# An expert's outputs added to the result: VectorE straight from PSUM, or a ScalarE copy and a GpSimd addition

## What is computed

```python
def moe_swiglu(h, router, w_gate_up, w_down):      # h: 256 tokens x 1024
    logits = hf @ router
    top_v, top_i = lax.top_k(logits, 2)
    gates = jax.nn.softmax(top_v, axis=-1)
    combine = sum(one_hot(top_i, 8) * gates[..., None])
    for e in range(8):                             # D_FF_EXPERT = 3584
        gate, up = split(hf @ w_gate_up[e])
        out = out + combine[:, e:e+1] * ((silu(gate) * up) @ w_down[e])
x = layer_norm(ALPHA * x + out + ple, ln2_g, ln2_b)
```

## Time and profile before

| | us |
|---|---|
| median of 3 runs | 1656.19 (1654.77 to 1656.62) |
| profiled execution, its time | 1656.22 |
| profiled execution, its span | 1654.0 |
| PE busy | 1591.2 (96% of the span) |
| DVE busy | 1356.8 (82%) |
| ACT busy | 979.7 (59%) |
| POOL busy | 164.3 (10%) |

### The profile page before, as it was taken

One profiled execution on the slowest core, in us unless ns is written; L12 is line 12 of the kernel. 1 busy time (PEld: TensorE's weight loads), 2 busy tenths in 40 slices (PEclk: granted clock), 3 DMA queues, 4 the chain that ended last, 5 costly groups with the idle time before them and its releaser, 6 DMA issues.

```text
span 1654.0 us, 24270 instructions
## 1 busy us (share of the span) xinstructions
PE 1591.2 (96%) x9080; PEld 1353.3 (82%) x9080; DVE 1356.8 (82%) x1301; ACT 979.7 (59%) x856; POOL 164.3 (10%) x151
## 2 busy tenths in 40 slices
PE   7999899999899988999999999999999999999996
PEld 5889689998889967888888888888888888888884
DVE  8976756655578777998998998998998998998997
ACT  3324434344545435777677777777777777677773
POOL 4000229950300010000000000000000000000000
PEclk9999999999999989999999999999999999999998
DMA  7434845554334566999999999999999999999992
GB/s 249 152 104 152 292 159 190 193 178 144 110 111 140 200 240 213 361 374 341 347 371 340 345 375 335 346 371 336 353 366 337 352 366 343 335 379 341 351 367 80
DMA packets 168560, 456.44 MB, mean 276 GB/s; under 512 B 7910, under 2 KB 60167, under 8 KB 167992
## 3 DMA queue, kind: packets, MB, share of 16 engines
q1 hardware_dynamic: 167736, 450.91, 75.9%
q0 software_dynamic: 768, 4.75, 0.8%
HBM read 453.01 MB, written 2.62 MB: 275 GB/s over the span
## 4 chain that ended last, share of the span: by engine, by line
PE 84%; DVE 9%; issue 3%; ACT 2%; POOL 1%; DMA 1%; DVEq 0%; SPq 0%; POOLq 0%; ACTq 0%
PE psum L667 20%; PE psum L668 19%; PE psum L669 19%; PE psum L674 5%; PE psum L676 5%; PE psum L675 5%; PE psum L762 5%; DVE wl L424 2%; PE psum L735 2%; PE psum L1107 1%; ACT wh L418 1%; PE psum L787 1%; POOL small L1507 1%; DVE xa L2064 1%; DVE ring_split L424 1%
## 5 line engine op out<-in xcount | busy, mean ns | idle before, releaser
L418 ACT ACTIVATE wh<-ring 128x2048 fp32r<-128x2048 f32 x379 | 724.5, 1923 | 228.7 <-PE psum L669 184.9
L424 DVE TENSOR_TENSOR wl<-ring,wh 128x2048 fp32r<-128x2048 f32 x341 | 772.1, 2290 | 87.9 <-ACT wh L418 80.4
L667 PE MATMUL psum<-wh,xgh 128*128 128x512 f32 x896 | 359.1, 401 | 8.9 <-DVE wl L424 8.9
L669 PE MATMUL psum<-wh,xgl 128*128 128x512 f32 x896 | 349.7, 390 | 0.0
L668 PE MATMUL psum<-wl,xgh 128*128 128x512 f32 x896 | 349.4, 390 | 0.0
L667 PEld LDWEIGHTS psum<-wh,xgh 128*128 128x128 f32 x896 | 168.2, 188 | 54.6 <-DVE wl L424 22.3
L667 PE MATMUL psum<-wh,hidh 128*128 128x512 f32 x536 | 209.7, 391 | 1.6 <-DVE ring_split L424 1.6
L669 PE MATMUL psum<-wh,hidl 128*128 128x512 f32 x536 | 208.7, 389 | 0.0
L669 PEld LDWEIGHTS psum<-wh,xgl 128*128 128x128 f32 x896 | 168.1, 188 | 36.6
L668 PEld LDWEIGHTS psum<-wl,xgh 128*128 128x128 f32 x896 | 168.5, 188 | 32.2
L668 PE MATMUL psum<-wl,hidh 128*128 128x512 f32 x448 | 174.3, 389 | 0.0
(11 more groups left out here) (377 smaller groups left out, 2149.9 us busy)
## 6 DMA issues: line engine op xcount, KB each, us to landing
ring<-in_moe_gu SPq DMA_DIRECT2D x224, 1024.0 KB, 6.8
ring<-in_moe_dn SPq DMA_DIRECT2D x112, 1024.0 KB, 7.1
ring<-in_w_in SPq DMA_DIRECT2D x26, 1024.0 KB, 5.4
ring<-in_w_gu SPq DMA_DIRECT2D x22, 1024.0 KB, 5.1
ring<-in_w_dn SPq DMA_DIRECT2D x11, 1024.0 KB, 4.9
ring<-in_w_out SPq DMA_DIRECT2D x8, 1024.0 KB, 6.6
ring<-in_w_pg SPq DMA_DIRECT2D x8, 1024.0 KB, 5.0
ring<-in_w_ba SPq DMA_DIRECT2D x4, 1024.0 KB, 5.1
```

Source lines behind the costliest of these rows:

```text
L418: eng.activation(parts(u)[0], ring[:, ring_slot(u), :], ACT.Copy).then_inc(hi_ready, 1)
L424: eng.tensor_tensor(lo, ring[:, ring_slot(u), :], hi.bitcast(F32), ALU.subtract).then_inc(lo_ready, 1)
L667: pe.matmul(dst, ah, bh, start=first, stop=False, skip_group_check=True)
L669: return pe.matmul(dst, al, bh, start=False, stop=last, skip_group_check=True)
```

## The change

ScalarE copies each of the four scattered products out of PSUM into a new SBUF buffer `spread_out` (128 x 2 x 1024, at the place of the transposed input `xT`), releases the bank after each copy, and stands with these copies at the end of its pass, behind the splits u0[2] to g1[1] and ahead of g1[2] of the next pass. GpSimd adds a block of 128x1024 to `xa` when both copies of the block are there, in a loop of its own over the passes, one addition waiting for the one before. VectorE's four additions go, and it waits for `out_added` ahead of the last layer norm. The semaphore `outer_added` keeps its name in the code, and its releases come from ScalarE now.

```diff
+        spread_out = place("spread_out", [P, NB, D], at=xT_at)
@@ semaphores
+        out_copied, out_added = sem("spread_out_copied"), sem("spread_out_added")
-        spread_full, outer_added = sem("spread_out_full"), sem("expert_out_added")
+        spread_full, outer_added = sem("spread_out_full"), sem("outer_banks_free")
@@ ScalarE, expert(it, last)
+                act.wait_ge(res_ready, 2)
                 split_used(act, ends[("d", ESTEPS - 1)] + 1, lap)
                 for o in range(2):
                     act.activation(yeh[:, o * 512:(o + 1) * 512], bank[2 + o][:, :], ACT.Copy, scale=slot_gate).then_inc(ye_hi, 1)
                 if not last:
                     some_hi("u", 0, 2, 4, it, order_ahead), some_hi("g", 1, 0, 2, it + 1)
+                x = ESTEPS if last else ESTEPS + 2
+                act.wait_ge(out_added, NB * it + 1)
+                for o in range(2):
+                    b = slot_group(x + 1 + o, it)
+                    act.activation(spread_out[:, 0, o * 512:(o + 1) * 512], b[:, :], ACT.Copy).then_inc(out_copied, 1)
+                    act.wait_ge(out_copied, 2 * NB * it + o + 1)
+                    act.nop().then_inc(x_free[(x + 1 + o) % 2], 1)
+                for o in range(2):
+                    act.wait_ge(spread_full, 2 * it + o + 1)
+                    act.activation(spread_out[:, 1, o * 512:(o + 1) * 512], bank[2 + o][:, :], ACT.Copy).then_inc(out_copied, 1)
+                    act.wait_ge(out_copied, 2 * NB * it + NB + o + 1)
+                    act.nop().then_inc(outer_added, 1)
@@ GpSimd
+            def add_outputs(it):
+                for b in range(NB):
+                    pool.wait_ge(out_copied, 2 * (NB * it + b + 1))
+                    pool.tensor_tensor(xa[:, b, :], xa[:, b, :], spread_out[:, b, :], ALU.add).then_inc(out_added, 1)
+                    pool.wait_ge(out_added, NB * it + b + 2)
             pool.wait_ge(pass_ready, 1)
+            pool.wait_ge(res_ready, 2)
+            pool.nop().then_inc(out_added, 1)
+            more = pool.value_load(npass[0:1, 0:1], min_val=NE - 1, max_val=2 * NE - 1)
+            with pool.Fori(0, more) as it:
+                add_outputs(it)
+            add_outputs(more)
             root(3)
@@ VectorE, expert(it, last)
-                for o in range(2):
-                    g = x + 1 + o
-                    dve.wait_ge(x_full, it * SLOT_GROUPS + g + 1 + EARLY)
-                    part = xa[:, 0, o * 512:(o + 1) * 512]
-                    link(dve.tensor_tensor(part, bank[5 + g % 2][:, :], part, ALU.add))
-                    dve.nop().then_inc(x_free[g % 2], 1)
-                for o in range(2):
-                    dve.wait_ge(spread_full, 2 * it + o + 1)
-                    part = xa[:, 1, o * 512:(o + 1) * 512]
-                    dve.tensor_tensor(part, bank[2 + o][:, :], part, ALU.add).then_inc(outer_added, 1)
@@ VectorE, behind the passes
-            dve.wait_ge(outer_added, 2 * more + 3)
+            dve.wait_ge(out_added, NB * (more + 1) + 1)
```

More of the change, by code:

```diff
@@ L2078, in _ @@
             more = dve.value_load(npass[0:1, 0:1], min_val=NE - 1, max_val=2 * NE - 1)
-            per_item = 2
-            n0 = c.n
             with dve.Fori(0, more) as it:
-                c.n, c.base = n0, it * per_item
                 expert(it, False)
-            assert c.n == n0 + per_item
-            c.n, c.base = n0, more * per_item
             expert(more, True)
-            dve.wait_ge(outer_added, 2 * more + 3)
+            dve.wait_ge(out_added, NB * (more + 1) + 1)
             c.sem, c.n, c.base = final_step, 0, 0
```

## The result

| | us |
|---|---|
| after, median of 4 runs | 1666.93 (1665.47 to 1668.41) |
| before, the four runs beside it | 1655.93 (1654.77 to 1656.62) |
| after to before | 1.0068, interval 1.0056 to 1.0080 |
| profiled execution after, its time (span) | 1665.47 (1663.4) |
| profiled execution before, its time (span) | 1656.22 (1654.0) |

The account below looks back on a forecast made before the run. The prediction took TensorE, 84% of the 1654.0 us, to bound the kernel. Passes 9.9 us plus end 3.7 us made 13.6 us on 1656.19, so 1669.8 us, range 1661 to 1678.

Parts of the forecast that it names:

- The mechanism: At the pass boundary, GpSimd's second addition holds off VectorE's low half of g1[2]; TensorE starts g1[2] 1.42 us later.
- The passes: Seven boundaries between passes, each with TensorE 1.42 us later at g1[2] and not won back: 9.9 us.
- the start of addition 1: GpSimd's second addition of a pass, forecast from 1039.95 to 1042.35 on the trace's time scale.
- The copies alone: At the pass boundary, ScalarE's copies delay the split of g1[2]; without any lock TensorE starts 0.25 us later.
- The end: After the eighth pass nothing hides the copies and additions: layer norm 3.7 us later, ends 3.0 and 4.6.
- seven equal steps of 121.6 us: First addition of the first pass to that of the eighth, 851.4 us, read as equal passes with TensorE idle 0.9 each.
- The gain side: VectorE's four additions go, 2.96 us a pass; on TensorE's path worth at most the 0.29 us wait before g1[2].
- The rival of a freed VectorE: Less VectorE work gives back at most TensorE's idle 0.9 us a pass: 1653.6 us, chance 0.07.
- No clash of the readers: GpSimd's additions do not meet VectorE's low half; only copies and the end cost, 5.5 us: 1661.7 us, chance 0.17.
- The clock in the passes: TensorE's 1.71 us stand before g1[2] halves its clock: 2.4 us a unit, 1686.6 us in all seven passes, chance 0.08.
- Not slower: Copies done sooner and GpSimd not holding VectorE: 6.3 us back in seven passes, less 3.7 at the end, chance 0.07.
- That it does what it says: Rival that GpSimd's additions become the bound themselves; the prediction held that two of 2.4 us in 121.6 cannot.

Follow-up runs that it names:

- a_no_additions: The changed kernel without GpSimd's sixteen additions, copies, waits and releases kept: 1656.81 us, 1.0005 to the kernel before.
- b_write_only: The changed kernel with each GpSimd addition replaced by a read of eight columns and two memsets that only write: 1661.66 us.
- d_last_on_vector: The changed kernel, but in the last pass VectorE adds the four products straight from PSUM, without that pass's copies and GpSimd additions: 1662.92 us.
- c_split_before_copies: The changed kernel with ScalarE's split of g1[2] moved ahead of its four copies: 1662.71 us.
- g_both: The changed kernel with g1[2] split ahead of ScalarE's copies and the last pass's additions on VectorE from PSUM: 1659.74 us.
- f_before_reordered: The kernel before, with VectorE's low half of g1[2] moved between its first two additions and its last two: 1656.38 us.
- i_vector_adds_behind_split: The changed kernel with g1[2] split before the copies, VectorE adding them behind its low half of g1[2], last pass from PSUM: 1651.76 us.
- e_vector_adds_copies: The changed kernel, but VectorE instead of GpSimd adds ScalarE's copies from SBUF at the end of its pass: 1657.55 us.
- h_twice_the_reading: The changed kernel with a second GpSimd addition of the same size, into a dead buffer, ahead of each: 1693.45 us.

## Why the prediction was right, point by point

**The mechanism held.** The wait before g1[2] was to be 1.7 us and is 1.44; the low half was to take near 3.5 us and takes 3.2 (5.42 less the second one's 2.2); GpSimd's addition was to take 2.4 us and takes 2.41; the copies 0.60 us, and 0.60 they are. That the additions carry most of the cost of a step and the copies little is shown by a_no_additions (0.93 against 0.19 us). That it takes GpSimd's reading is shown by b_write_only, as far as a memset can stand for an addition that doesn't read. And a_no_additions keeps all the waits and releases, so they are not the cause. The estimate for a size without a row, along the slope of two rows with the same kind of operands, was right to 0.01 us; the row with the broadcast input would have misled.
The Trainium skill's rule (SBUF — State Buffer, "SBUF: two separate sides") holds in these traces as to who excludes whom: a GpSimd operation that only writes left VectorE's 2.29 us alone, one that reads did not. Its whole exclusion is again slightly more than is seen: the low half began 1.07 us before the addition's end and grew by 0.93.

**The sizes.** *The passes*, forecast 7 x 1.42 = 9.9 us, came to 7.87. The mis-sized term is the start of addition 1: from the scatter's first pair (its second matmul at 1036.20) it came 4.45 us later, and I had 4.73. I took 0.26 for the self-wait between ScalarE's first two copies, and it is 0.18; 0.16 for GpSimd's reaction, and it is 0.08 (1038.00 to 1038.08); 0.28 for its self-wait, and it is 0.16. That is 0.28 us a pass of the 0.30 between 1.42 and the 1.12 measured. *The copies alone*, forecast 0.25 us a step, are 0.19. Their last self-wait, at the end of the loop's body, took 0.59 us where I had 0.26; the others, 0.18 and 0.12, were shorter and paid for it.

*The end*, forecast 3.7 us, is 2.74 in the profiled pair. The two aren't alike, though: the last scatter ran at a granted clock of 0.50 before and of 1.00 after. With equal clocks the runs give 3.81 us (after and d_last_on_vector, full) and 3.28 (c_split_before_copies and g_both, half). The kernel before itself had half clock, and against its 4.35 us c_split_before_copies gives 3.32. How long its end would be at full clock no run shows, as d_last_on_vector adds without its self-waits. The forecast assumed half clock, so its term was 0.4 us too long: in c_split_before_copies GpSimd reacts after 0.07 us and not 0.16, waits for itself 0.16 and not 0.28, adds in 2.35 and 2.34 us and not 2.40, and VectorE follows after 0.03 and not 0.1. That the profiled pair shows less than either is the accident of the clock.

**A reading that was wrong.** I called the stretch from the first addition of pass one to that of pass eight seven equal steps of 121.6 us. They are six of 125.1 and one of 101.3: the last pass has no next expert to gather and to start. So the 123.0 us that I named for the new step could not come; it is 126.25. The sum didn't use it, as it multiplies a delay by seven boundaries. The 0.9 us of idleness a pass came from the same mean: an ordinary pass has 0.61 us (125.10 less 124.49 busy), and the stand of 2.30 us before the last scatter made up most of the rest. A mean over a window shows a period only if the rows in it are seen to be equally spaced.

**The gain side.** I held that the four additions cost TensorE at most the 0.29 us wait. But the wait that is listed is not the whole lateness: g1[2] starts 0.89 us after the turn in the kernel before (1042.25 and 1043.14) and 0.35 us after it where nothing is late (1042.39 and 1042.74, above), so it was 0.54 us late; the modelled length of the turn hides the rest. And the 3.1 us in ten waits are not all at the boundary: each pass has two, the second 82 us behind the scatter, in the timeline of TensorE before:

```profile
1116.84 0.50 PE L667 MATMUL psum<-wh,xgh 128*128 128x512 f32 x1 [0.32 <-DVE wl L424]
```

It stays in every variant (0.31 to 0.34 us) and is no part of the result. f_before_reordered shows that the lateness at g1[2] is not a cost of the additions' place but of VectorE's work up to the first down unit, and i_vector_adds_behind_split that 0.6 us a pass were to be had there. The rival of a freed VectorE was right that something is there, and short of it in this kernel because the freed time was spent waiting for ScalarE (3.10 us).

**The rivals.** No clash of the readers (1661.7 us): refuted, the wait was 1.44 and not 0.5 us. The clock in the passes: not seen, granted 1.00 through them after and also with twice the reading. Not slower: refuted for this order of work. That it does what it says: it does.

## What to carry to other kernels

Moving an addition from PSUM on VectorE to SBUF on GpSimd does not only take load off VectorE: it makes a second reader of SBUF. In these runs every VectorE operation with two SBUF inputs that met it was late by nearly what GpSimd still had to do, and so was the next one where GpSimd had had to wait. What did better here was to put ScalarE's copies behind the split that TensorE needs next, and to leave the sum on VectorE in a gap of its own. Measure a late unit by where it starts, not by the wait that is listed before it. When a wait disappears from one place and the period stays, look for it a few units on; and a chain of three engines that hides under the next pass stands bare after the last one.

## What was not expected of the hardware

**One stand, two clocks.** TensorE stands 2.30 us before the last scatter in the kernel before and after. Before, the clock was at 0.50 behind it; after, at 1.00, by the scatter's row and the window (length, busy of PE, PEld, DVE, ACT, POOL; clock, DMA):

```profile
1643.40 0.49 PE L1166 MATMUL psum<-yeh,spread 128*128 128x512 f32 x1 [2.30 <-DVE yel L2084]
...
1643.40:1645.30 1.90, 1.90 (x8) 1.42 (x8) 0.00 (x0) 0.95 (x2) 0.00 (x0) 1.00 0.00 0
```

c_split_before_copies and g_both show the scatter at half clock behind the same 2.30 us; a_no_additions, b_write_only, e_vector_adds_copies and d_last_on_vector show it at full clock. In f_before_reordered, h_twice_the_reading and i_vector_adds_behind_split the clock fell within the scatter, 0.3, 0.8 and 0.8 us behind its start. So a stand of this length can end either way, and the scatter's matmuls stand 0.43 or 0.23 us apart for it. Its length alone does not settle the clock, as I had taken it to when I set the two stands of 1.82 and 2.30 us side by side.

**Turns.** Where both engines have readers waiting, they alternate operation by operation: GpSimd's 2.41 us became 4.24 and 4.46 (h_twice_the_reading), 3.94 and 4.36 us (c_split_before_copies).
